# Constant matmuls at eight places where TensorE waits, in a one-core diffusion-layer kernel

## The reference

```
mod = silu(cond) @ w_ada + b_ada               # two condition rows; 6 x 1024 columns
h   = LN(x) * (1 + scale1) + shift1
p   = h @ w_in                                 # split into attention and GLA q/k/v, gates ...
merged = gate_a * (attention @ w_br_attn) + gate_g * (gla @ w_br_gla)
x   = LN(alpha*x + g1 * (merged @ w_out))
h2  = LN(x) * (1 + scale2) + shift2
group, experts = top-1 of 4 groups, top-2 of 8 experts, from h2 @ router weights
y   = sum over the 32 experts of weight * (silu(h2 @ gate_e) * (h2 @ up_e)) @ down_e
x   = LN(alpha*x + g2 * y)
```

## Time and profile before

| | |
|---|---|
| median of three runs | 731.15 us |
| the profiled execution | 733.35 us |
| its span in the trace | 731.6 us |
| TensorE (PE) busy | 612.3 us, 84% of the span |
| weight loads (PEld) busy | 336.4 us |
| VectorE / ScalarE / GpSimd busy | 244.3 / 113.1 / 115.4 us |
| mean granted TensorE clock | 0.927 |
| moved by DMA | 176.93 MB |

### The profile page before, as it was taken

The page is one execution under the profiler, slowest core; times in us unless marked ns, Lnnn a source line. Parts: engine busy times, 40 slices in busy tenths (PEclk is TensorE's granted clock), DMA queues, the critical chain, the costliest instruction groups (busy, mean ns, idle before and its releaser), DMA issues.

```text
span 731.6 us, 8001 instructions
## 1 busy us (share of the span) xinstructions
PE 612.3 (84%) x3161; PEld 336.4 (46%) x3161; DVE 244.3 (33%) x497; ACT 113.1 (15%) x230; POOL 115.4 (16%) x118
## 2 busy tenths in 40 slices
PE   1799999999999999999999945999997887788500
PEld 0274345554444455564444544666654444445200
DVE  2421543236744543132236862111111111111146
ACT  0020252210022221124000011111110110001010
POOL 3000000020200000000002212233332223211133
PEclk9769999999999999999999955999999999999955
DMA  9977444136432030239954293899999999999352
GB/s 334 369 227 242 163 176 168 63 115 233 136 116 83 32 116 11 105 114 324 394 198 176 86 394 129 345 406 405 405 404 408 404 403 401 404 405 381 122 191 86
DMA packets 67320, 176.93 MB, mean 242 GB/s; under 512 B 10372, under 2 KB 12324, under 8 KB 67280
## 3 DMA queue, kind: packets, MB, share of 16 engines
q1 hardware_dynamic: 50976, 144.42, 51.9%
q10 hardware_dynamic: 10560, 23.68, 9.0%
q0 software_dynamic: 5744, 8.28, 3.3%
HBM read 174.87 MB, written 11.96 MB: 255 GB/s over the span
## 4 chain that ended last, share of the span: by engine, by line
PE 66%; DMA 16%; SPq 6%; DVE 5%; issue 3%; POOL 2%; ACT 1%; POOLq 0%; DVEq 0%
PE bank L1441 23%; PE bank L1688 10%; DMA X<-exp_w_up 8%; PE bank L1613 6%; PE bank L1627 6%; PE bank L1696 4%; DMA W<-exp_w_up 3%; DMA X<-w_ada 3%; SPq L430 3%; PE bank L1393 2%; PE bank L1571 2%; PE bank L1589 2%; SPq L440 1%; PE bank L1494 1%; PE bank L1674 1%
## 5 line engine op out<-in xcount | busy, mean ns | idle before, releaser
L1441 PE MATMUL bank<-W,Y 128*128 128x512 f32 (+1 forms) x432 | 183.2, 578 | 0.0
L1441 PEld LDWEIGHTS bank<-W,Y 128*128 128x128 f32 x432 | 81.0, 192 | 85.3 <-issue 82.6
L1688 PE MATMUL bank<-X,Y 128*64 128x256 f32 x704 | 86.7, 402 | 19.7 <-DMA X<-exp_w_up 18.1
L1688 PEld LDWEIGHTS bank<-X,Y 128*64 128x64 f32 x704 | 56.0, 145 | 56.9 <-DMA X<-exp_w_up 27.8
L615 POOL TENSOR_TENSOR rstd<-ss,cst 128x1 f32<-128x1 f32 (+3 forms) x21 | 25.5, 1214 | 319.4 <-DVE ss L771 319.4
L1134 DVE COPY abias<-bank 128x128 f32<-128x128 f32 x32 | 9.3, 291 | 132.9 <-PE bank L1726 132.9
L659 POOL DMA_INDIRECT Y<-h_rows,gidx x32 | 32.7, 1022 | 120.0 <-PE bank L1674 92.5
L664 POOL DMA_INDIRECT pair_rows<-PTr,sidx x32 | 32.4, 1013 | 78.8 <-DVE PTr L1140 78.8
L1688 PE MATMUL bank<-W,Y 128*64 128x256 f32 (+1 forms) x320 | 37.0, 348 | 8.9 <-DMA Y<-exp_w_up 6.1
L1696 PE MATMUL bank<-X,abias 128*64 128x512 f32 x176 | 42.6, 602 | 1.2 <-DVE abias L1134 0.8
L1140 DVE COPY PTr<-bank 128x512 f32<-128x512 f32 x32 | 22.1, 691 | 60.5 <-PE bank L1696 60.5
(11 more groups left out here) (204 smaller groups left out, 654.2 us busy)
## 6 DMA issues: line engine op xcount, KB each, us to landing
X<-exp_w_gate SPq DMA_DIRECT2D x22, 1024.0 KB, 16.4
X<-exp_w_up SPq DMA_DIRECT2D x22, 1024.0 KB, 19.9
X<-exp_w_down SPq DMA_DIRECT2D x22, 1024.0 KB, 19.7
W<-w_in SPq DMA_DIRECT2D x8, 2048.0 KB, 8.5
Y<-w_ada ACTq DMA_DIRECT2D x8, 2048.0 KB, 9.2
W<-exp_w_gate SPq DMA_DIRECT2D x10, 1024.0 KB, 16.4
W<-exp_w_up SPq DMA_DIRECT2D x5, 1024.0 KB, 19.8
W<-exp_w_down SPq DMA_DIRECT2D x5, 1024.0 KB, 20.2
```

The source lines that it names most:

```text
L1441: ins = mm(bank[:, 0:cols], hT[:, i, k, :], w[:, k, :], start=k == 0, stop=k == KT - 1)
L1688: ins = mm(bank[hh * 64:hh * 64 + 64, a:b], x_[:, c, h * 64:h * 64 + 64], rhs(hh), start=k == 0 and a == 0, stop=k == KT - 1, skip_group_c ...
```

## The change

A helper `keep_busy(count)` issues `count` calls of `mm` with the identity constant as stationary operand and the first 512 columns of the constants as moving operand, into bank 6, which nobody reads at that time. It waits for nothing and tells nobody. It is called at eight places: before modulation block 0 (11 calls, behind the wait for the constants), before blocks 1, 2 and 3 (15, 6 and 6), before the transposes of the last tile in the second norm (8), after the router's matmuls (11), after the counts (4), and after the index tables, before the first gathered tokens (11). These are 72 calls. No other instruction changes or moves.

```diff
+FILL_START = (11, 15, 6, 6)
+FILL_NORM, FILL_ROUTER, FILL_RANK, FILL_GATHER = 8, 11, 4, 11
...
+            def keep_busy(count):
+
+                for _ in range(count):
+                    mm(banks[6][:, :], ident, cst[:, 0:HALF], start=True, stop=True)
+
             pe.wait_ge(S["consts_in"], 16)
+            keep_busy(FILL_START[0])
             pe.wait_ge(S["cond_silu"], 2)
             colbank = side.claim(pe, "modc", 0)
             for n in range(4):
+                if n:
+                    keep_busy(FILL_START[n])
                 modulation(n)
                 if n:
                     columns(colbank, 8 * (n - 1), n - 1)
...
             for i in range(TILES):
+                if i == TILES - 1:
+                    keep_busy(FILL_NORM)
                 second_transposes(i)
...
             main.filled(ins, "router")
+            keep_busy(FILL_ROUTER)
             pe.wait_ge(S["both_ready"], 1)
...
             side.filled(ins, "count")
+            keep_busy(FILL_RANK)
             main.wait_read(pe, "wo", 0, TILES - 1)
...
             index_tables(0)
+            keep_busy(FILL_GATHER)
             next_tokens(0)
```

## The result

The changed kernel takes 750.42 us in the median of four runs, the kernel before 730.56 beside it: ratio 1.0258, 95% interval 1.0228 to 1.0287, slower. A second measurement of the same two kernels gave 1.0254 (1.0227 to 1.0281). The forecast was slower, 746.0 us with a range of 739 to 751; the sign, the two places and the mechanism hold, the size was 4.4 us short.

A forecast was written before the change was run, and what follows sets the result against it. The prediction took weight loads to bound the start, TensorE the long middle and DMA the experts. Start 10.1 plus second part 4.8 gave 14.9 us on the median 731.15: 746.0 us, range 739 to 751.

The forecast's parts named there:

- The price of a call: Each added constant matmul call on TensorE costs 0.86 us at 2.4 GHz and twice that at 1.2 GHz.
- The rival of cheap calls: At all eight runs a call costs 0.43 us, so waits end as now: 13 us faster, 718; 7 in 100.
- The start, 10.1 us: Calls before modulation blocks 0 to 3 make block 4 begin 10.1 us late: 13.2 lost, 3.1 given back.
- the clock's rise: In the first 11 calls, before block 0, 4.5 us run at 1.2 GHz, adding 2.2 us; bounds 1.7 and 2.6.
- What the higher clock gave back: From the first transposes into the first projection, the 2.4 GHz clock returns 3.1 us of the start's loss.
- since TensorE has no gap: After the start's runs the clock stays at 2.4 GHz because TensorE has no gap; this returns 3.1 us.
- The first projection "near 55": In the changed profile the first projection after the modulation blocks should begin near 55 us.
- The second part, 4.8 us: From last norm to first gather and expert 0: 8.1 us lost at four runs, 3.3 given back, 4.8 late.
- The middle passes all on: Between block 4 and the norm no DMA is in the chain, so the start's 10.1 us moves on whole.
- The experts pass all on: SyncE's weight load follows expert 0's gate and up, so d us later there moves the end d us.
- The sum: Whole kernel: 10.1 + 4.8 = 14.9 us on a span of 731.6, so 748.3 profiled and a median of 746.0.
- the step down: The profiled execution was 2.2 us above the median, so 14.9 was added to the median 731.15, giving 746.0.

The follow-up runs named there:

- experiment 3: Changed kernel with all eight runs' counts kept but each call 256 moving columns wide instead of 512; ratio 0.9898 to the kernel before.
- experiment 4: Changed kernel with about half the full-width calls: 6, 8, 3, 3 at the start, 4, 6, 2, 6 from norm to gather; ratio 0.9882 to the kernel before.
- experiment 2: Changed kernel with only the calls before modulation blocks 0 to 3 (11, 15, 6, 6), none later; 745.59 us against 732.95 for the kernel before, ratio 1.0174.
- experiment 11: The changed kernel measured again without edit, beside the kernel before; ratio 1.0254.
- experiment 6: Changed kernel with no calls at the start and 4, 6, 2, 6 from the last norm to the first gather; ratio 0.9899 to the kernel before.
- experiment 5: Changed kernel with 6, 8, 3, 3 calls before modulation blocks 0 to 3 and none later; ratio 0.9983 to the kernel before.
- experiment 7: Changed kernel with no calls at the start, 4, 6, 2 from norm to counts and none before the gathered tokens; ratio 0.9945 to the kernel before.
- experiment 8: Changed kernel with only 6 calls, ahead of the first gathered tokens, and none elsewhere; ratio 0.9973 to the kernel before.
- experiment 1: Changed kernel without the calls before blocks 0 to 3, keeping 8, 11, 4, 11 later; 736.58 us against 732.95 for the kernel before, ratio 1.006.

## Why the prediction was right

**The price of a call** (0.86 us at 2.4 GHz, from 48 calls of the same form). Right: in the second part 8 calls took 6.95 us, 11 took 9.52 and 9.50, 4 took 3.52. The rival of cheap calls is out, and experiments 3 and 4 show that its counts would have been the right ones at half the price. Their gain is 7 to 9 us rather than its 13. In their profiles the second part gains 7.1 and 6.9 us where it had 7.5; the start gains 2.3 and 2.8 where it had 5.5, since that sum ignored when the weights of blocks 3 and 4 and of the first projection land; and middle and experts take 2.8 and 0.7 us back. The Trainium skill's four passes for true float32 ("FP8 and Floating Point Precision", "TensorE Precision Notes") and its 216 ns for 512 columns ("TensorE: Matmul & The Clock Gate", "Back-to-back issue gap") give an estimate of 0.864 us a call; the trace agrees at 0.864 (9.50 for 11).

**The start, 10.1 us.** Measured 11.1. The step that was small is the clock's rise: I took 4.5 us at 1.2 GHz with bounds of 3.5 and 5.1 from two places. In the changed kernel the first 11 calls took 12.65 us, 3.2 more than at 2.4 GHz, so the low clock lasted about 6.4 us, outside my bounds. In experiment 2 the same calls took 11.10 us, so 3.3 us at the low clock, and in experiment 11 11.98 us, so about 5. The time to rise varies from execution to execution, and two readings were too few for bounds. What the higher clock gave back was 3.5 us where I had 3.1. That it stays up "since TensorE has no gap" held in the profiles of the changed kernel and of experiment 2, and not in that of 11. The first projection "near 55" was a slip of mine: my own terms give about 57, and it began at 57.83.

**The second part, 4.8 us.** Measured 4.3. As I had taken it, the clock did not fall where it fell before, at 423.4; transposes and router took 3.1 and not 3.3, ranks and counts 1.26 and not 1.4.

**The middle passes all on.** Right to 0.1 us, in the profile. In those of experiments 2, 3 and 6 the middle was 1.0 to 1.2 us longer; why was not looked at.

**The experts pass all on.** Nearly: 274.2 us from SyncE's load to the end against 273.2. In the other profiles it is 273.7 to 275.1, without a relation to the runs, so the 273.2 of before, the lowest of all, may be what is odd. What makes up that 1 us stays open; no experiment looked at it.

**The sum.** For the profiled execution I had 748.3 us and it took 749.75: +1.0 start, -0.5 second part, +1.0 experts. The rest of the miss, 2.9 us, is the step from this pair of executions to the medians. I took 2.2 us off because the profiled execution of before was that much above its median, and so took the difference of the pair, 14.9, for the difference of the medians. It was not: the profiles differ by 16.4 us, the medians by 19.9, and by 19.7 in experiment 11. That step failed.

One reason is shown in part. The kernel before varies with its clock: in the 29 runs of it beside experiments 5 to 8 (727.2 to 735.8 us) the 16 with a mean granted clock of 0.924 or less averaged 733.5 us, the 13 above it 730.3. That mean is of the whole execution and does not say where. The profiles do for one place: that of before began its first projection at 45.49 us in the timeline; that of experiment 1, where the start is the same program, at 42.42, with block 2 already at 2.4 GHz:

```profile
26.09 1.92 PE L1397 MATMUL bank<-X,csil 128*32 128x512 f32 x16 [0.30 <-DMA X<-w_ada]
...
42.42 9.48 PE L1453 MATMUL bank<-W,Y 128*128 128x288 f32 x32
```

What the runs give back at the start was priced against an execution in which the clock was low for long; against a middling one it is less, by about 1.7 us if the other four profiles with this start are taken (experiments 1, 6, 7 and 8: block 4 at 52.9 us on the mean, against 54.57). The second part varies too: in experiment 2 it is the program of before and took 34.3 us, not 35.8, because the clock rose again within gate and up of expert 0 (5.06 us, not 6.44). But the changed kernel is not free of such luck: its start came out at 65.69, 67.22 (experiment 11) and 64.20 us (experiment 2). Without the step down the forecast would have been 748.3, 2.1 below the measured median. That the whole 2.2 us is luck in the one profile of before is argued and not shown; that the two parts together cost more than each by itself is not excluded either.

## What to carry to other kernels

Work that is put into a wait has to be shorter than the wait, so take its price from the same form of instruction, by calls and not by records: here a call was two records, and counts that fit at 0.43 us cost 0.86. Count the part of a run that falls into the low clock at twice its price: at the start 11 calls took 12.65 us, against 9.50 in the second part. Keep the clock only where what follows is the bound: after the router it was worth 7 us in the profiles, ahead of loads that land on their own time nothing that could be measured. And when the clock differs from execution to execution, take the difference from several executions of the kernel before; one profile, shifted to the median, does not give it.

## What the runs showed of the hardware that was not expected

The rise of TensorE's clock under the same dense calls took about 3.3 us in one execution, 5 in another and 6.4 in a third. It can also fall without a long wait: in experiment 11 it fell at about 54 us, with no idle stretch of TensorE above 0.57 us in the 12 us before, and in the first profile of the same program it stayed up through an idle 0.82 us at that place. Before the first clock record the page shows 1.00 whatever the clock is: block 0 of the kernel before took 3.64 us under that 1.00, and block 4, the same 16 records, 1.92 us after a rise.

A merged row of the timeline takes in the waits between its instructions. ScalarE's queue in the profile of before reads like this (start, us, line, operands, count):

```profile
16.45 20.38 ACTq L1189 DMA_DIRECT2D abias<-b_ada  x4
36.87 0.63 ACTq L1193 DMA_DIRECT2D Y<-w_ada  x1
```

It looks as if four rows of bias, 4 KB each, held the queue for 20 us. In narrow windows they are four issues of 0.24 us:

```profile
16.45 0.24 ACTq L1189 DMA_DIRECT2D abias<-b_ada  x1
25.38 0.24 ACTq L1189 DMA_DIRECT2D abias<-b_ada  x1
30.29 0.24 ACTq L1189 DMA_DIRECT2D abias<-b_ada  x1
36.60 0.24 ACTq L1189 DMA_DIRECT2D abias<-b_ada  x1
```

The last stands behind the end of block 3 (32.11 + 3.64 = 35.75 us), for whose bank ScalarE waits in the program. So block 4's weights are asked for late because of that wait, not because the issues are slow. An issue can be slow, though: single requests for `W<-w_in` held SyncE's queue for 3.74, 7.50 and 3.52 us, at 17.31, 21.09 and 28.64 us, while the DMA engines were full (busy share 1.05 from 17 to 32 us).
